# Odd block and last attention pair: another order of the products, no phase borders for TensorE, and GpSimd makes nine low weights

## The reference

```python
z = h @ p["w_in"]
u, g = jnp.split(z, [W_POOL], axis=-1)
d = multiscale_pool(...u...)              # 4 groups of 512 columns, window 2, 4, 8, 16
y = jnp.einsum("bngi,gij->bngj", d, p["w_grp"]) * p["scale"]
out = (y * jax.nn.silu(g)) @ p["w_out"]

logits = q @ k.T * scale + c[t] - c[s]    # 16 heads of 64, causal
probs = jax.nn.softmax(jnp.where(mask, logits, -jnp.inf), axis=-1)
o = (probs @ v) * jax.nn.silu(g)
h = h + o @ w_out
```

## Time and profile before

| | us |
|---|---|
| median of 3 runs | 3169.97 (3166.43 to 3172.95) |
| the profiled execution | 3172.45 |
| its span, first to last instruction | 3170.3 |
| PE busy | 2962.7 (93%) |
| DVE busy | 1746.6 (55%) |
| POOL busy | 1316.3 (42%) |
| ACT busy | 1088.0 (34%) |
| mean granted TensorE clock | 0.973 of full speed |

### The profile page before, as it was taken

One profiled execution on the slowest core, in us unless ns is written; L12 is line 12 of the kernel. 1 busy time (PEld: TensorE's weight loads), 2 busy tenths in 40 slices (PEclk: granted clock), 3 DMA queues, 4 the chain that ended last, 5 costly groups with the idle time before them and its releaser, 6 DMA issues.

```text
span 3170.3 us, 40111 instructions
## 1 busy us (share of the span) xinstructions
PE 2962.7 (93%) x13930; PEld 2287.7 (72%) x13930; DVE 1746.6 (55%) x2284; ACT 1088.0 (34%) x1429; POOL 1316.3 (42%) x1638
## 2 busy tenths in 40 slices
PE   5999999989999999989899999998999999997997
PEld 3688888757788777867688877776667666665775
DVE  7688999955545116534632322535555655556353
ACT  5344444342211000001332221324455555665232
POOL 2344454447644434436422324775221121211575
PEclk9999999999999999999899999999999999999999
DMA  7412222344311321113301103333222212221423
GB/s 298 161 63 64 63 76 73 114 151 162 102 49 44 116 80 37 47 39 137 107 27 34 33 27 106 96 87 131 54 47 54 48 33 48 48 34 41 140 82 111
DMA packets 113294, 258.56 MB, mean 82 GB/s; under 512 B 24624, under 2 KB 38000, under 8 KB 112384
## 3 DMA queue, kind: packets, MB, share of 16 engines
q1 hardware_dynamic: 83456, 189.43, 20.5%
q10 hardware_dynamic: 29696, 67.21, 5.9%
HBM read 223.97 MB, written 32.64 MB: 81 GB/s over the span
## 4 chain that ended last, share of the span: by engine, by line
PE 75%; DVE 11%; ACT 6%; POOL 4%; issue 3%; DMA 2%; DVEq 0%; POOLq 0%; SPq 0%; ACTq 0%
PE ps L660 20%; PE ps L661 19%; PE ps L662 19%; POOL t_wl L590 3%; PE ps L1212 2%; PE ps L1229 1%; DVE ps L2117 1%; PE ps L1027 1%; PE ps L1028 1%; PE ps L1029 1%; POOL t_wh L585 1%; DVE t_ptl L2580 1%; PE ps L1249 1%; ACT t_pr L1848 1%; DVE t_pb L2327 1%
## 5 line engine op out<-in xcount | busy, mean ns | idle before, releaser
L660 PE MATMUL ps<-t_h_hi,t_wh 128*128 128x512 f32 x2464 | 1011.6, 411 | 43.9 <-POOLq L593 13.5
L585 POOL CAST t_wh<-t_wst 128x1024 fp32r<-128x1024 f32 (+2 forms) x306 | 313.6, 1025 | 1712.1 <-PE ps L662 1538.9
L661 PE MATMUL ps<-t_h_lo,t_wh 128*128 128x512 f32 x2464 | 982.7, 399 | 0.0
L662 PE MATMUL ps<-t_h_hi,t_wl 128*128 128x512 f32 x2464 | 981.9, 398 | 0.0
L590 POOL TENSOR_TENSOR t_wl<-t_wst,t_wh 128x256 fp32r<-128x256 f32 (+2 forms) x1224 | 926.1, 787 | 24.5
L660 PEld LDWEIGHTS ps<-t_h_hi,t_wh 128*128 128x128 f32 x2464 | 467.8, 190 | 196.7 <-issue 60.5
L661 PEld LDWEIGHTS ps<-t_h_lo,t_wh 128*128 128x128 f32 x2464 | 469.0, 190 | 112.7 <-issue 8.5
L662 PEld LDWEIGHTS ps<-t_h_hi,t_wl 128*128 128x128 f32 x2464 | 467.6, 190 | 112.2
L2117 DVE SCALAR_TENSOR_TENSOR ps<-t_upad,t_vec,ps 128x1024 f32<-128x1024 f32 x224 | 275.5, 1284 | 7.1 <-DVE ps L2111 0.9
L660 PE MATMUL ps<-t_y_hi,t_wh 128*128 128x512 f32 x512 | 208.4, 407 | 21.7 <-DVEq L264 14.6
L661 PE MATMUL ps<-t_y_lo,t_wh 128*128 128x512 f32 x512 | 205.6, 402 | 0.0
(11 more groups left out here) (350 smaller groups left out, 4267.4 us busy)
## 6 DMA issues: line engine op xcount, KB each, us to landing
t_wst<-w_even_in SPq DMA_DIRECT2D x40, 512.0 KB, 3.5
t_wst<-w_ple SPq DMA_DIRECT2D x64, 320.0 KB, 2.9
t_wst<-w_even_out SPq DMA_DIRECT2D x32, 512.0 KB, 3.6
t_wst<-w_fox_in SPq DMA_DIRECT2D x32, 512.0 KB, 3.6
...
```

Of the source, the lines that this page charges most:

```text
L585: pool.tensor_copy(wh[b][:, 0:w], wst[b][:, 0:w]).then_inc(S("w_high"), 1)
L660: pe.matmul(o, w1, x1, start=start and k == 0, stop=False)
L661: pe.matmul(o, w1, x2, start=False, stop=False)
L662: last = pe.matmul(o, w2, x1, start=False, stop=stop and k == kts - 1)
```

## The change

**Odd block.** The eight tiles behind `u` are taken in the order of `ODD_ORDER` (0 is a product of `h`, 1 one of `d`): h, h, d, d, h, d, h, d instead of h, d, h, d, h, d, h, d. SP's addresses, TensorE's products and the waits of ScalarE and VectorE follow. TensorE no longer waits at the borders `oout_a`, `odd_b` and `oout_b`. Instead it waits for `o_y` (a slot's y is formed), for each y in turn (`y_ready`), and, ahead of the second part, for all eight residuals (`x_added`).

The diff, without most lines around it. Left out are hunks that only pass on the new order (waits of ScalarE and VectorE, `done` in `out_by_halves`, which skips the first two tiles) and ScalarE's wait for `f_pv` ahead of its high parts:

```diff
@@ -32,12 +32,18 @@
+ODD_ORDER = [(0, 0), (0, 1), (1, 0), (1, 1), (0, 2), (1, 2), (0, 3), (1, 3)]
+ODD_AT = [1024 * j for j in range(4)] + [4096 + 1536 * j + 1024 * kind for kind, j in ODD_ORDER]
+ODD_WIDTHS = [1024] * 4 + [(1024, 512)[kind] for kind, j in ODD_ORDER]
...
     ("w_even_out", 4, [1024] * 4),
-    ("w_odd_in_a", 2, [1024] * 4 + [1024, 512] * 4),
+    ("w_odd_in_a", 2, ODD_WIDTHS),
     ("w_odd_out_a", 4, [1024] * 2),
-    ("w_odd_in_b", 2, [1024] * 4 + [1024, 512] * 4),
+    ("w_odd_in_b", 2, ODD_WIDTHS),
     ("w_odd_out_b", 4, [1024] * 2),
@@ -198,7 +204,8 @@
             return bank(2 + t % 6 if t != 6 else 0)
-        return bank(t % 4)
+        return bank(6 + t if name == "fout" and t < 2 else t % 4)
@@ -382,6 +389,13 @@
+    EARLY = [(0, 0), (0, 1), (0, 2), (1, 0), (0, 3), (1, 1), (0, 4), (1, 2), (0, 5), (0, 6), (1, 3), (0, 7),
+             (1, 4), (1, 5)]
+    EARLY_AT = {9 + n: x for n, x in enumerate(EARLY)}
+    POOLED = 9
@@ -515,6 +529,9 @@
                     store_max(times - 1, c)
+                    if c == 1:
+                        for j in range(2):
+                            load_tile("w_fox_out", 0, j, j * T, T, (T, T))
                     load_max(times - 1, c)
@@ -543,9 +560,14 @@
             for half in range(passes(name)):
+                if name == "w_fox_out" and half == 0:
+                    with sp.Fori(0, times - 1) as i:
+                        for j, w in enumerate(widths):
+                            load_tile(name, i + 1, j, j * T, w, widths)
+                    continue
                 with sp.Fori(0, times) as i:
                     for j, w in enumerate(widths):
-                        load_tile(name, i, j, sum(widths[:j]) if name != "w_even_in" else EVEN_AT[j], w, widths,
+                        load_tile(name, i, j, ODD_AT[j] if name.startswith("w_odd_in") else sum(widths[:j]), w, widths,
                                   half * times * len(widths))
@@ -591,6 +613,25 @@
+        def last_pair():
+            for i in range(max(POOLED, 9)):
+                if i < POOLED:
+                    c, b, q0, q1 = queries(i)
+                    x, n = 2 * (i % 2) + 1, q1 - q0
+                    pool.wait_ge(S("f_ph"), 24 * 7 + 2 * i + 2)
+                    pool.tensor_tensor(ptl[x][:, 0:n], pr[x][:, 0:n], pth[x][:, 0:n].bitcast(F32),
+                                       ALU.subtract).then_inc(S("f_pl2"), 1)
+                if 1 <= i <= 8:
+                    k = i - 1
+                    pool.wait_ge(S("f_y"), 4 * k + 2)
+                    pool.tensor_copy(hcol(h_hi, 0, k), hcol(yf, 0, k)).then_inc(S("yf_high"), 1)
+                    pool.wait_ge(S("yf_high"), k + 1)
+                    pool.tensor_tensor(hcol(h_lo, 0, k), hcol(yf, 0, k), hcol(h_hi, 0, k).bitcast(F32),
+                                       ALU.subtract).then_inc(S("yf_ready"), 1)
@@ -622,6 +663,16 @@
             for half in range(passes(name)):
+                if name == "w_fox_out" and half == 0:
+                    for j, w in enumerate(widths):
+                        split_tile(name, 0, j, w, widths, 0)
+                    pool.wait_ge(S("w_used"), first[name] + 2)
+                    last_pair()
+                    with pool.Fori(0, times - 1) as i:
+                        for j, w in enumerate(widths):
+                            split_tile(name, i + 1, j, w, widths, 0)
+                    continue
                 with pool.Fori(0, times) as i:
...
@@ -956,6 +1009,10 @@
+        def y_ready(part, k):
+            pe.wait_ge(S("o_gs"), 8 * part + 2 + k + 1)
@@ -972,16 +1029,16 @@
                     project(j % 2, slot(j), h_hi, h_lo).then_inc(S("w_used"), 1)
-                for j in range(4):
-                    a, b = 2 * j % 4, (2 * j + 1) % 4
-                    act((9, 11, 13, 14)[j])
-                    take(nm, i, 4 + 2 * j)
-                    project(0, slot(a), h_hi, h_lo).then_inc(S("w_used"), 1)
-                    act(10) if j == 0 else act(12) if j == 1 else yev(3 + j)
-                    take(nm, i, 5 + 2 * j)
-                    if j == 0:
-                        pe.wait_ge(S("o_d"), 4 * g + 4)
-                    project(1, slot(b), d_hi, d_lo, kts=4).then_inc(S("w_used"), 1)
+                for n, (kind, j) in enumerate(ODD_ORDER):
+                    take(nm, i, 4 + n)
+                    if kind == 0:
+                        act((9, 11, 13, 14)[j])
+                        project(n % 2, slot(2 * j % 4), h_hi, h_lo).then_inc(S("w_used"), 1)
+                    else:
+                        act(10) if j == 0 else act(12) if j == 1 else yev(3 + j)
+                        if j == 0:
+                            pe.wait_ge(S("o_d"), 4 * g + 4)
+                        project(n % 2, slot((2 * j + 1) % 4), d_hi, d_lo, kts=4).then_inc(S("w_used"), 1)
             if part == 0:
@@ -991,21 +1048,20 @@
-        def out_phase(nm, ready, stat, after, operand=(y_hi, y_lo)):
-            with pe.Fori(0, 4) as i:
-                out_pair(nm, i, [(*operand, ready)], "x_added", 2)
+        def out_phase(part, nm, after):
+            out_pair(nm, 0, [(y_hi, y_lo, lambda k: y_ready(part, k))], "x_added", 2)
+            with pe.Fori(0, 3) as i:
+                out_pair(nm, i + 1, [(y_hi, y_lo, None)], "x_added", 2)
             pe.wait_ge(S("w_used"), first[after] + 2)
-            if stat is not None:
-                stats(stat)
             end(pe)
...
         odd_groups(0)
-        begin(pe, "oout_a")
-        out_phase("w_odd_out_a", None, None, "w_odd_in_b")
-        begin(pe, "odd_b")
+        pe.wait_ge(S("o_y"), 4 * 1 + 7)
+        out_phase(0, "w_odd_out_a", "w_odd_in_b")
+        pe.wait_ge(S("x_added"), 2 + KT)
         odd_groups(1)
-        begin(pe, "oout_b")
-        out_by_halves("oout_b", "w_odd_out_b", lambda c: None, (y_hi, y_lo))
+        pe.wait_ge(S("o_y"), 4 * 3 + 7)
+        out_by_halves("oout_b", "w_odd_out_b", lambda c: (lambda k: y_ready(1, k)) if c == 0 else None, (y_hi, y_lo))
@@ -1236,7 +1292,11 @@
             c, b, q0, q1 = queries(i)
-            at_least("f_pl", 24 * p + 2 * i + 2)
+            if isinstance(p, int) and p == 7:
+                pe.wait_ge(S("f_pl"), 24 * p + 2 * i + 2 - min(i + 1, POOLED))
+                pe.wait_ge(S("f_pl2"), min(i + 1, POOLED))
+            else:
+                at_least("f_pl", 24 * p + 2 * i + 2)
             if i == 0:
@@ -1269,6 +1329,18 @@
+        def early_out(t, ks):
+            base = first["w_fox_out"]
+            if ks[0] == 0:
+                pe.wait_ge(S("f_g"), 8)
+                pe.wait_ge(S("w_split"), base + t + 3)
+            last = project(wbuf("w_fox_out", t), None, h_hi, h_lo, chunks=[(0, HALF, out_bank("fout", t))], ks=ks,
+                           ready=(lambda k: pe.wait_ge(S("yf_ready"), k + 1)) if t == 0 else None)
+            if ks[-1] == KT - 1:
+                last.then_inc(S("w_used"), 1)
@@ -1286,6 +1358,8 @@
                     turn_values(p, like)
+                if attend and not project_more and h in EARLY_AT:
+                    early_out(EARLY_AT[h][0], (EARLY_AT[h][1],))
                 if attend and h % 2 == 1 and h > 1:
@@ -1304,8 +1378,11 @@
         end(pe)
-        begin(pe, "fout")
-        out_by_halves("fout", "w_fox_out", lambda c: lambda k: pe.wait_ge(S("yf_ready"), 8 * c + k + 1), (h_hi, h_lo))
+        early_out(1, (6, 7))
+        pe.wait_ge(S("f_add"), 24 * 8)
+        out_by_halves("fout", "w_fox_out", lambda c: lambda k: pe.wait_ge(S("yf_ready"), 8 * c + k + 1), (h_hi, h_lo),
+                      done=2)
         ple(1, "fout")
...
@@ -1908,10 +1987,9 @@
         begin(act, "fout")
-        for c in range(2):
-            for k in range(KT):
-                A(hcol(h_hi, c, k), hcol(yf, c, k), ACT.Copy).then_inc(S("yf_high"), 1)
         load_x(x_d)
+        for k in range(KT):
+            A(hcol(h_hi, 1, k), hcol(yf, 1, k), ACT.Copy).then_inc(S("yf_high"), 1)
         act.wait_ge(S("yf_ready"), 16)
...
@@ -2562,7 +2640,12 @@
             dve.wait_ge(S("f_st"), NU * p + i + 1)
-            at_least("f_pv", NU * p + i - 1)
+            if not (isinstance(p, int) and p == 7):
+                at_least("f_pv", NU * p + i - 1)
+            elif i > 1:
+                dve.wait_ge(S("f_pl"), 24 * p + 2 * i - 2 - min(i - 1, POOLED))
+                dve.wait_ge(S("f_pl2"), min(i - 1, POOLED))
             if b == 0:
@@ -2574,7 +2657,7 @@
             n = q1 - q0
-            for hh in range(2):
+            for hh in range(1 if isinstance(p, int) and p == 7 and i < POOLED else 2):
                 x = 2 * (i % 2) + hh
@@ -2603,7 +2686,7 @@
             for h in range(24):
-                if attend and h % 2 == 0:
+                if attend and h % 2 == 0 and (project_more or h == 0):
                     add_scores(p, h // 2, like)
@@ -2620,6 +2703,8 @@
                         values_low(p, like)
+                    if h % 2 == 1 and not project_more and h < 23:
```

(12 more changed lines are left out.)

12 lines of the change are left out of this document (8 added, 4 removed).

## The result

| | kernel before | changed kernel |
|---|---|---|
| median, us | 3171.46 (3166.43 to 3173.81) | 3146.39 (3143.47 to 3150.3) |
| the profiled execution, us | 3172.45 | 3145.53 |
| its span, us | 3170.3 | 3143.8 |
| mean granted TensorE clock | 0.973 | 0.975 |

The ratio is 0.9924, 95% interval 0.9907 to 0.9941: faster by 25 us, where 48 were forecast, and outside the predicted range. TensorE's busy time is 2961.1 us against 2962.7, so all of it is idle time and clock.

What follows compares the result with a forecast made beforehand. TensorE, busy 93% of 3170.3 us, was taken as the bound, with its idle time and clock to win. Odd block 41.9 plus last pair 6 made 48 us: 3122 for the median, 3124.5 for the profiled execution, range 3107 to 3138.

Steps and rivals of the forecast that it cites:

- (a): Border into the odd block's first output phase: idle time 4.72 and 1.9 of clock go, 6.6 us won.
- (b): Into the odd block's second part: TensorE waits for the last residual, not the store of x; 5.0 us won.
- (e): Border into the odd block's second output: 4.44 idle and 3.1 of clock, less 0.2 for handover; 7.3 us won.
- rival 2: Borders only change their name: waits of 2 to 3 us remain, clock keeps falling; gain 34, 3136 us, chance 0.12.
- (c): Odd block's third group: the extra `h` product covers the 7.71 us idle time fully; 10.8 us won.
- (d): Odd block's fourth group: 2.7 of 13.94 us stay idle, 1 us of clock comes back; 12.2 us won.
- the load in front of (f): Last pair: the weight load issued behind the store of the last maxima takes 4.5 us, landing at 2885.5.
- (f): Last pair: GpSimd makes second-head low weights in units 0 to 8, 1.4 us each, and the first half's output columns.
- (g): Last pair: VectorE adds scores of unit i+1 ahead of unit i's low weights; wins nothing in units 4 to 8.
- rival 3: GpSimd becomes the bound of the last pair, making it slower: 3179 us at 11 us per unit; chance 0.03.
- (h): Last pair: 16 early output projection steps (11.2 us) fill TensorE's idle time; the output border's 6.29 us goes.
- x and the first residual: Fifth output tile: x, loaded first, takes some 8.3 us at most, the residual 0.7; the tile starts at 2956.4.

Runs made afterwards that it cites:

- run 3: Changed kernel with SyncE issuing the first two output weight loads ahead of both stores of the last pair's maxima: 3128.3 us, ratio 0.9871.
- run 7: Changed kernel with early weight loads, VectorE making both heads' low weights in all units, none on GpSimd: 3133.9 us, ratio 0.9888.
- run 8: Changed kernel with early loads and additions as before, first two output tiles in one piece behind the last unit: 3124.2 us, ratio 0.9852.
- run 6: Changed kernel with VectorE's additions back in their old place: 3134.6 us with late weight loads, 3122.4 us with early ones.

## Why the prediction was wrong, step by step

- **(a), (b), (e), the borders:** right in kind, each idle time went as far as said (0.41, 1.90, 0.30). Predicted 18.9, measured 16.0 alone. The borders did not change their name (rival 2).
- **(c), (d), the order:** (c) has no wait left, (d) 3.31 in place of 2.7, and its clock fell as it had fallen behind the 13.94: 0.83 over the next 10 us both times, 1.7 us lost, so that nothing of it came back where I had taken 1. Predicted 23.0, measured 19.6 alone. Together 36.3 for 41.9: 5.6 us of the miss, a matter of size. The 10 us behind the wait in the kernel before (us, busy of each engine, clock, DMA share, GB/s; in the changed kernel TensorE is busy 9.94 of 10 there, and the clock 0.83 too):

```profile
1368.30:1378.30 10.00, 10.00 (x36) 8.01 (x37) 2.51 (x3) 0.00 (x0) 2.36 (x5) 0.83 0.00 0
```

- **The failed step is the load in front of (f):** "with the queue empty I take 4.5". The queue was not empty, since the store of the last maxima was issued 1 us before. It took 14.05 us to the first tile. The splits were cheaper than taken (8.0 for 10.0), and GpSimd's low part of 128x512 took 1.28 for the 1.4 taken. Unit 0's values waited 21.7 us for the 13 forecast and came at 2866.66, in the old frame 2904.8 and not 2897.0. Taking the load out of that place gave 18.1 us back (run 3), more than the 9.5 of the mis-sized term, since it also takes away the wait that I had foreseen. The hint lay in the kernel before, in the landing of its 32 stores of maxima. (The 12.3 us from the store to its broadcast are no measure of it, since the broadcast also waits for `shared`, which ended at 2892.37, just ahead of it.)

```profile
DMA to landing us min/median/max: 6.6/8.9/11.1
```

- **The whole miss of the last pair** is 15.7 us at the fifth output tile (2972.1 in the old frame, forecast 2956.4): 7.8 at unit 0, 2.8 from there to unit 4 (20.4 for 17.6), 1.0 from unit 4 to unit 8 (20.3 for 19.3), 4.1 behind unit 8 (26.6 for 22.5).
- **(g), the additions one unit ahead:** said to win nothing; it costs 5.9 us with early loads and 11.8 with late ones (6.5 and 7.6 from the store to the end). The prediction named its consequence, `shared` and the broadcast behind the addition of unit 2, and put the price in, but as part of a stall rather than as a part of the change that could be left out. Per unit 5.06 us instead of 4.8.
- **(f):** GpSimd was not the bound (rival 3), and its share is worth some 5 us once its queue is clear, as far as run 7 tells. The rule on the shared read port of the Trainium skill ("Perfetto Trace Analysis", "Optimizing Scalar/DVE Operations") shows in single rows, below, and doesn't turn the sign.
- **(h):** right in kind, as far as is known. The times of run 8 can't tell whether the 11.2 us of steps won anything; its trace has 8.1 us at the fifth tile, the 11.2 less the wait behind them.
- **x and the first residual:** 8.3 us from issue to use were taken, it was 10.4 (issued 2922.73, used 2933.17). But x was not what ended last. VectorE's low parts of the second half's columns, 7.9 us of work ahead of that addition in the same queue, had no term in the sum; they kept VectorE until 2932.5, and x added 0.67 us.

3122 us was reached by the kernel with both steps undone (run 6), with another sum: of the 47.8 us in its round 36 are the odd block's and some 12 the last pair's, instead of 42 and 6. That the totals meet is chance.
